# A two-layer hybrid decoder step: block order at three stage starts, and the last squares of a norm summed on PE

## What is computed

```
def _rmsnorm(x, g):
    return x * rsqrt(mean(x * x) + 1e-6) * g
h = _rmsnorm(x, norm_mix_pre)
z = h @ w_in                       # 55 tiles of 128 columns
m = sigmoid(ga) * (ya @ w_out_a) + sigmoid(gb) * (yb @ w_out_b)
x = x + _rmsnorm(m @ w_o, norm_mix_post)
h = _rmsnorm(x, norm_ffn_pre)
f = (silu(h @ w_ffn_gate) * (h @ w_ffn_up)) @ w_ffn_down
x = x + _rmsnorm(f, norm_ffn_post)
```

## Time and profile before

| | us |
|---|---|
| median of 3 runs | 1325.74 |
| lowest and highest | 1322.05, 1326.98 |
| profiled execution, its own time | 1322.61 |
| its span, first to last instruction | 1320.8 |
| PE busy | 1248.3 (95%) |
| DVE, ACT, POOL busy | 866.6, 545.4, 108.2 |
| mean granted PE clock | 0.978 |

### The profile page before, as it was taken

The page is one execution under the profiler, slowest core; times in us unless marked ns, Lnnn a source line. Parts: engine busy times, 40 slices in busy tenths (PEclk is TensorE's granted clock), DMA queues, the critical chain, the costliest instruction groups (busy, mean ns, idle before and its releaser), DMA issues.

```text
span 1320.8 us, 27667 instructions
## 1 busy us (share of the span) xinstructions
PE 1248.3 (95%) x11984; PEld 1174.5 (89%) x11984; DVE 866.6 (66%) x1460; ACT 545.4 (41%) x821; POOL 108.2 (8%) x124
## 2 busy tenths in 40 slices
PE   6999989999998999999989997999999989999996
PEld 5898877899997999999888986879989979999996
DVE  4887558777676566554477873578777656666533
ACT  5552334354445433343444533353434454333432
POOL 0004163000000000000000050720000000000000
PEclk9999989999998999999989999999999989999998
DMA  6433135544453544544423323264444534444541
GB/s 223 128 114 114 52 100 162 176 160 143 136 153 107 183 147 147 154 153 150 143 87 121 117 96 79 71 213 156 144 144 136 160 99 140 160 144 145 158 146 70
DMA packets 51177, 179.50 MB, mean 136 GB/s; under 512 B 6257, under 2 KB 7025, under 8 KB 49777
## 3 DMA queue, kind: packets, MB, share of 16 engines
q1 hardware_dynamic: 41904, 150.49, 36.3%
q10 hardware_dynamic: 9152, 27.25, 6.2%
HBM read 166.57 MB, written 8.53 MB: 133 GB/s over the span
## 4 chain that ended last, share of the span: by engine, by line
PE 83%; DVE 10%; issue 3%; ACT 3%; ACTq 1%; DMA 0%; SPq 0%; DVEq 0%
PE dense L1297 51%; PE core L1297 32%; DVE w_lo L841 2%; ACT w_hi L547 1%; DVE x L889 1%; DVE y_out L887 1%; ACTq L681 1%; DMA x<-x_t 0%; DVE s_gate L1104 0%; DVE s_st L1086 0%; DVE bonus L952 0%; DVE s_st L1087 0%; DVE u_exp L1031 0%; DVE y_a L1151 0%; DVE tmp L938 0%
## 5 line engine op out<-in xcount | busy, mean ns | idle before, releaser
L841 DVE TENSOR_TENSOR w_lo<-w_raw,w_hi 128x1024 fp32r<-128x1024 f32 x282 | 348.8, 1238 | 238.0 <-ACT w_hi L547 237.2
L547 ACT ACTIVATE w_hi<-w_raw 128x1024 fp32r<-128x1024 f32 x282 | 298.0, 1057 | 481.9 <-PE dense L1297 335.3
L1297 PE MATMUL dense<-h_hi,w_hi 128*128 128x320 f32 x1296 | 421.7, 325 | 26.1 <-DVE h_lo L845 14.5
L1297 PE MATMUL dense<-h_lo,w_hi 128*128 128x320 f32 x1296 | 407.1, 314 | 0.0
L1297 PE MATMUL dense<-h_hi,w_lo 128*128 128x320 f32 x1296 | 407.0, 314 | 0.0
L1297 PEld LDWEIGHTS dense<-h_hi,w_hi 128*128 128x128 f32 x1296 | 249.4, 192 | 43.6 <-issue 31.6
L1297 PEld LDWEIGHTS dense<-h_lo,w_hi 128*128 128x128 f32 x1296 | 249.9, 193 | 2.0 <-issue 0.2
L1297 PEld LDWEIGHTS dense<-h_hi,w_lo 128*128 128x128 f32 x1296 | 249.2, 192 | 0.0
L1297 PE MATMUL core<-h_hi,w_hi 128*128 128x320 f32 x416 | 129.8, 312 | 0.0
L1297 PE MATMUL core<-h_hi,w_lo 128*128 128x320 f32 x416 | 129.3, 311 | 0.0
L1297 PE MATMUL core<-h_lo,w_hi 128*128 128x320 f32 x416 | 129.3, 311 | 0.0
(11 more groups left out here) (293 smaller groups left out, 1974.9 us busy)
## 6 DMA issues: line engine op xcount, KB each, us to landing
w_raw<-wts SPq DMA_DIRECT2D x282, 512.0 KB, 3.5
ret_t<-ret_t ACTq DMA_DIRECT2D x16, 256.0 KB, 3.8
ret_s<-ret_t ACTq DMA_DIRECT2D x16, 256.0 KB, 2.4
ret_rest<-ret_d ACTq DMA_DIRECT2D x2, 1536.0 KB, 7.6
qk_rot<-qk_raw ACTq DMA_DIRECT2D x8, 320.0 KB, 6.5
dmask<-rconst ACTq DMA_DIRECT2D x2, 1152.0 KB, 7.1
s_st<-wkv_st ACTq DMA_DIRECT2D x2, 1024.0 KB, 6.0
wkv_s<-s_st ACTq DMA_DIRECT2D x2, 1024.0 KB, 4.4
```

What stands on the lines that cost most here:

```text
L547: act.activation(w_hi[n % RING][:, :], w_raw[n % RING][:, :], ACT.Copy).then_inc(hi_ready.sem, 1)
L841: dve.tensor_tensor(w_lo[r][:, :], w_raw[r][:, :], w_hi[r][:, :].bitcast(F32), ALU.subtract).then_inc(low_made.sem, 1)
L1297: return pe.matmul(out, lhsT, rhs, start=start, stop=stop)
```

## The change

1. **Sums of a norm.** DVE adds seven squares only. PE sums `acc` and then, in a second matmul into the same bank, the eighth square itself. On ACT the `high` behind block 7 moves behind the root. On DVE the `low` of block 7 moves from before the wait for the root to behind the third group of `x`, and `h_lo` of blocks 2 and 3 is made in that place too, one group earlier than before.
2. **Feed-forward.** In the first four cycles of each layer PE takes block k for groups 0, 2, 1, 3 and then block k+1 for the four.
3. **Layer 1's opening** has an order of its own: blocks 0 to 3 of tiles 0 and 1 in turn, blocks 0 to 3 of tile 2, blocks 4 to 7 of tile 0, both sums, blocks 4 to 6 of tile 1, the pick, its block 7, and blocks 4 to 7 of tile 2. Layer 0's and W_OUT_B's orders are written as a list too and stay as they were.
4. **Tile 3 of layer 1.** ACT makes its `w_hi` between the two waits of the root, DVE its `w_lo` before it waits for the root.

```diff
+OPEN_FIRST = [(step - 2 * i, i) for step in range(12) for i in range(3) if 0 <= step - 2 * i < 8]
+OPEN_FIRST[6:6] = [("sum", 0), ("sum", 1)]
+OPEN_FIRST[11:11] = [("pick", 0)]
+OPEN_NEXT = [(k, i) for k in range(4) for i in range(2)] + [(k, 2) for k in range(4)] + [(k, 0) for k in range(4, 8)] \
+    + [("sum", 0), ("sum", 1), (4, 1), (5, 1), (6, 1), ("pick", 0), (7, 1)] + [(k, 2) for k in range(4, 8)]
...
                 def x_root(k):
                     act.wait_ge(*x_partial(layer, k))
                     act.activation(acc[:, :], core[0][:, 0:T], ACT.Copy).then_inc(x_parted.sem, 1)
+                    if k == 1 and layer:
+                        high(RING)
                     act.wait_ge(*x_summed(layer, k))
...
-                        high(after(c))
+                        if c < KT - 1:
+                            high(after(c))
+                    norm_root(k)
+                    high(after(KT - 1))
...
                         dve.wait_ge(*y_squared(layer, (k - 1) * KT + c + 1))
-                        if c:
+                        if 0 < c < KT - 1:
...
-                        for n in lows(c):
-                            low(*n)
+                        if c < KT - 1:
+                            for n in lows(c):
+                                low(*n)
                     dve.wait_ge(*rooted(layer, k))
...
                         if after:
-                            while done < lo:
+                            while done < (hi if i == 2 else lo):
                                 after(done)
                                 done += 1
+                            if i == 2:
+                                for n in lows(KT - 1):
+                                    low(*n)
...
-                    low(layer, j + RING)
+                    if j or not layer:
+                        low(layer, j + RING)
...
+                if layer:
+                    low(layer, RING)
                 dve.wait_ge(*x_rooted(layer, 1))
...
                 def norm_sum(k):
                     pe.wait_ge(*squares(layer, k))
-                    mm(core[0][:, 0:T], ones, acc[:, :]).then_inc(sum_done.sem, 1)
+                    mm(core[0][:, 0:T], ones, acc[:, :], True, False)
+                    pe.wait_ge(*y_squared(layer, k * KT))
+                    mm(core[0][:, 0:T], ones, ch(sq8, KT - 1), False, True).then_inc(sum_done.sem, 1)
...
-                    for ph, one in enumerate((0, 2, 1, 3)):
-                        if k0 == 0:
+                    both = [(one, k) for one in (0, 2, 1, 3) for k in (k0, k0 + 1)]
+                    if ready:
+                        both.sort(key=lambda u: u[1])
+                    for one, k in both:
+                        if k == 0:
                             open_bank(g + one)
```

More of the change, by code:

```diff
@@ L29 @@
 FIRST_WEIGHTS = (0, 2, 3)
-SUMS_AT = (4, 6)
+OPEN_FIRST = [(step - 2 * i, i) for step in range(12) for i in range(3) if 0 <= step - 2 * i < 8]
[3 more added lines that the diff above has]
+    + [("sum", 0), ("sum", 1), (4, 1), (5, 1), (6, 1), ("pick", 0), (7, 1)] + [(k, 2) for k in range(4, 8)]
 X_GROUP_OF = [i for i, (a, b) in enumerate(X_GROUPS) for _ in range(a, b)]
@@ L135 @@
 FILL = (2, 2, 1)
-ACT_STEPS, DVE_STEPS, POOL_STEPS = 13, 221, 18
+ACT_STEPS, DVE_STEPS, POOL_STEPS = 13, 219, 18
 def program(nc, x_t, wts, pvec, lora, shift0, fixed, rmask, trig, rconst, wkv_st, ret_d, ret_t,
@@ L793, in _, with project_out @@
                 high(T_WO + 2 - 1)
-                def project_out(before, after, group0, gain):
+                def project_out(before, after, group0, gain, k):
                     for c in range(8):
@@ L802, in project_out @@
                         act.activation(ch(y_out, c), bank(g)[:, 0:T], ACT.Copy, scale=vec(gain, c)).then_inc(dense_evac_a.sem, 1)
-                        high(after(c))
+                        if c < KT - 1:
+                            high(after(c))
+                    norm_root(k)
+                    high(after(KT - 1))
                 for s in (shift_stored, wkvs_stored, wkvp_stored, retp_stored, *rets_stored):
                     act.wait_ge(*s(layer, s.per_layer))
-                project_out(lambda c: T_WO + c + 2, lambda c: T_WO + c + RING, G_WO, "mix_post")
-                norm_root(1)
+                project_out(lambda c: T_WO + c + 2, lambda c: T_WO + c + RING, G_WO, "mix_post", 1)
                 open_x(layer, 2, "ffn_pre", lambda c: act.wait_ge(*x_mixed(layer, X_GROUP_OF[c] + 1)))
@@ L825, in down_tile @@
                     return T_DOWN + (FK * (c + 1) - 1) // KT
-                project_out(lambda c: down_tile(c) + 2, lambda c: down_tile(c) + 3 if c == 7 else down_tile(c) + 2, G_DOWN, "ffn_post")
-                norm_root(2)
+                project_out(lambda c: down_tile(c) + 2, lambda c: down_tile(c) + 3 if c == 7 else down_tile(c) + 2, G_DOWN, "ffn_post", 2)
                 assert steps[0] == ACT_STEPS, steps
@@ L874, in norm_add @@
                         dve.wait_ge(*y_squared(layer, (k - 1) * KT + c + 1))
-                        if c:
+                        if 0 < c < KT - 1:
                             ins = dve.tensor_tensor(acc[:, :], ch(sq8, 0) if c == 1 else acc[:, :], ch(sq8, c), ALU.add)
-                            if c < KT - 1:
+                            if c < KT - 2:
                                 link(ins)
@@ L1354, in x_pick, with opening @@
                     mm(core[0][:, 0:T], pick, acc[:, :]).then_inc(x_summed.sem, 1)
[L1356 to L1379, removed]
+                def opening(j0, g0, ready, first, order):
+                    for k, i in order:
+                        j, g = j0 + i, g0 + i
+                        if k == "sum":
+                            x_sum(1, i)
+                            continue
+                        if k == "pick":
+                            x_pick(1)
+                            continue
+                        if k == 0:
+                            pe.wait_ge(*low_ready(layer, j))
+                            open_bank(g)
+                        if i == 0:
+                            pe.wait_ge(*ready(layer, first + k + 1))
+                        for n, (w, which) in enumerate(parts(j, k)):
+                            ins = mm(bank(g)[:, 0:T], w, ch((h_hi, h_lo)[which], k), k == 0 and n == 0, k == KT - 1 and n == 2)
+                        if k == KT - 1:
+                            ins.then_inc(tile_used.sem, 1)
+                opening(0, 0, h_ready, 0, OPEN_NEXT if layer else OPEN_FIRST)
                 pe.wait_ge(*lora_loaded(layer, 1))
@@ L1709, in _ @@
                                      for k in range(4)], ya_hi, ya_lo)
-                opening(T_WOB, G_WOB, yb_ready, 0)
+                opening(T_WOB, G_WOB, yb_ready, 0, [u for u in OPEN_FIRST if u[0] not in ('sum', 'pick')])
                 for c in range(RING, 8):
@@ L1719, in cycle @@
                     pe.wait_ge(*low_ready(layer, T_GU + n))
-                    for ph, one in enumerate((0, 2, 1, 3)):
-                        if k0 == 0:
-                            open_bank(g + one)
[L1723 to L1728, removed]
+                    both = [(one, k) for one in (0, 2, 1, 3) for k in (k0, k0 + 1)]
+                    if ready:
+                        both.sort(key=lambda u: u[1])
+                    for one, k in both:
+                        if k == 0:
+                            open_bank(g + one)
+                        if ready and one == 0:
+                            pe.wait_ge(*ready(layer, k))
+                        for m, (w, which) in enumerate(parts(T_GU + n, 4 * (k - k0) + one)):
+                            ins = mm(bank(g + one)[:, 0:T], w, ch(act[which], k), k == 0 and m == 0, k == last and m == 2)
+                        if k == k0 + 1:
+                            ins.then_inc(phase_done.sem, 1)
                 for q in range(FK // 2):
```

## The result

The kernel after takes 1313.5 us in the median of 4 runs (1311.33 to 1314.26), the kernel before 1325.9 (1322.05 to 1326.98) beside it. The ratio is 0.9922 with an interval from 0.9902 to 0.9941: 10.3 us, from 7.8 to 13.0. A second measurement with more runs gave 0.9926 (0.9909 to 0.9942), 9.8 us. The forecast was 7.0 us faster, or 1318.7 us, in a range from 1314.5 to 1323.0, and faster by over 0.5% was its likeliest case. The way was right.

What follows compares the result with a forecast made beforehand. PE bounds the kernel, busy 1248.3 of 1320.8 us, so gains lie where it stands still or runs slowly. 0.5 + 2.1 + 2.1 + 2.3 = 7.0 us off the 1325.74 median gives 1318.7, range 1314.5 to 1323.0.

Steps and rivals of the forecast that it cites:

- Start of the chain: Four norm ends: the sum of `acc` fits behind the last tile, so the second sum starts 0.52 us earlier at each.
- The gap in the feed-forward: Feed-forward starts: PE's wait for block 1, worth 1.19 us, goes; block 4 is in time with 1.9 us in hand.
- The clock's term: Feed-forward starts: clock rises 5.1 to 6.0 us after an earlier last restart; 2.1 us gained each, gap and earlier root included.
- My bounds, 0.9 and 2.35: Gain per feed-forward start: 0.9 us if the clock rises no earlier than before, 2.35 if 5.1 us after the restart.
- The opening: Layer 1's start: two gaps become one of 0.2 us and the clock rises earlier; gain 2.3 us, bounds 1.4 and 2.8.
- my own list: Signs for and against; the prediction is wrong if, among others, PE waits for `h_lo` of block 4 or later.
- rival (b): Moved `w_lo` delays DVE's blocks 4 to 7, `acc` sum doesn't fit; gain only 4.8 us, 1320.9; chance 0.17.
- The sum: Whole kernel: 0.5 (end) + 2.1 + 2.1 (feed-forward starts) + 2.3 (layer 1's opening) = 7.0 us faster.
- upper bound of 8.05: Whole kernel, largest gain: 0.55 + 2.35 + 2.35 + 2.8 = 8.05 us, or 1317.7 us.
- Rival (a): At the three starts the clock rises no earlier although PE runs without gaps; gain 3.7 us, 1322.0; chance 0.17.
- Rival (c): Stalls elsewhere now drop the clock; 16 us more slow time cancels the gain, 30 more give 1332; chance 0.04.
- The 20 us of slow time elsewhere: Slow clock outside the three starts, some 20 us now, would have to more than double for the kernel to become slower.

Runs made afterwards that it cites:

- without_sum: The kernel after with the norm's new sum and all that was moved with it put back; ratio to the kernel before 0.9944 (0.9922 to 0.9965).
- after_fill3: The kernel after with three matmuls that nobody reads added behind the norm's sum; ratio to the kernel before 0.9944 (0.9925 to 0.9962).
- open_alone: The kernel before with only layer 1's new opening order and tile 3's halves made before the root; ratio 0.9971 (0.9958 to 0.9984), 3.8 us.

## Why the prediction came out right, and where it was off

- **Start of the chain, right.** The root and `y_out` came 0.5 us earlier at each end; the sum of `acc` fit behind the last tile; the tail gave 0.52.
- **The gap in the feed-forward, right.** PE doesn't stop in the first cycles, and the `h_lo` of block 4 is 1.2 us early (1.9 forecast; it ends at about 423.8, and PE comes at 424.99).
- **The clock's term, right in direction, too small.** I took the clock to be low at PE's restart, as in the three places before, and to rise 5 to 6 us later. In the kernel after it fell only 1.35 us behind the restart (416.92 against 415.57), and was slow for 3.4 us instead of 10.2, all of it behind the restart, where I had 5.6. The start gained 3.2 us instead of 2.1; 0.45 x (5.6 - 3.41) = 1.0 is this difference. This is the term of the sum that was mis-sized. The second execution had 6.8 us of slow clock at the first start, 5.53 of it behind the restart, and gained 2.25 there, which is my figure. At full clock on either side the two orders, edit 1 included, are 24.43 - 22.85 = 1.58 us apart, more than the 1.15 at equal low clock, since the old order then waits longer for block 1 (1.29 us); the rest of 3.2 is clock. My bounds, 0.9 and 2.35, were too narrow above: they moved the rise and left the fall where it was, and the rise came earlier too, 4.75 us behind the restart and not 5.1 or more.
- **The opening, 2.65 for 2.3, inside its bounds.** I had seen that `h_lo` would set a floor, but put it at block 7 with 0.6 us in hand at block 4. The `h_lo` of block 4 came nearly when I said (8.2 us behind PE's restart, I had 8.4); PE was ready for it earlier (8.1, I had 9.0), and waited. By my own list a wait for block 4 was a sign of being wrong. It came true here, and it bounds this term.
- **Edit 1 is not worth 0.5 at every end.** It gave 0.52 at the tail and 0.5 at each feed-forward start at equal low clock, but not in layer 1. I had put the moved `w_lo` into DVE's chain and taken it to fit. It makes `h_lo` of block 4 come 1.25 us later against the cut than without edit 1, and so the opening can't be shorter than 48.4. With the old orders, where PE wants that block after 18 matmuls, it cost 1.2 us more than the kernel before there. This is the first half of rival (b)'s mechanism, hidden by the other gains; its second half, that the sum of `acc` doesn't fit, is refuted.
- **The sum.** 7.0 forecast; 9.5 by stretches. Of the 2.5 between them 2.2 are from the two feed-forward starts and 0.35 from the opening. That the sum lies beyond my upper bound of 8.05 and the time still near the range is luck in part: the range was widened by the spread of the runs.
- **Rival (a)**, a rise no earlier, is refuted: the clock rose 4.75 us behind the restart of the first start (420.32 - 415.57), 7.97 before (425.36 - 417.39), and all starts in the new order agree (3.7 to 5.5). **Rival (c)**, slow clock elsewhere, is real as an effect: the unchanged mixing stretch took 353.4 to 359.9 us, and this execution of the kernel after had 358.9, 2.5 more than before's. The clock was low for 13.7 us in that stretch then, for 10.2 us in before, and for 6.8 us in the second execution of the kernel after, which had 355.2. So this doesn't hang on the change. (The 20 us of slow time elsewhere that the prediction gives leave out some 8 us at the kernel's end.)

The Trainium skill (TensorE: Matmul & The Clock Gate, Part 1: The HAM clock gate) says that the moment of the clock's change isn't tied to the kernel. These runs agree: the same kernel's first feed-forward start had 3.4 us of slow clock in one execution and 6.8 in the other, 0.95 us apart.

What stays open: how much of the 10 us is edit 1's. The times say 0.9926 with it and 0.9944 without, 2.4 us with overlapping intervals, but from two measurements. The one measurement that has both kinds gives 0.9944 for without_sum and 0.9944 for after_fill3, whose stretches are those of the kernel after: nothing. The stretches say 1.2 us (0.6 + 0.6 + 0.5 - 0.5), or 1.8 (0.6 + 0.6 + 0.5 + 0.1) where the low clock in the opening is as long as in open_alone. No measured time shows edit 1's share.

## What to carry to other kernels

Where an engine restarts on pieces that arrive one by one, order its work so that the first pieces feed as many results as there are banks: it fills the gaps, and with TensorE's clock that pays twice. The matmul order of the feed-forward alone took 3.4 us off the time here. A step moved out of one wait lands in front of something else; follow that engine's queue to the piece that is wanted latest, not only past the first one. If TensorE must wait some microseconds before a dense stretch, matmuls that nobody reads can be cheaper than the wait, if they fill nearly all of it: six helped here and three did not.

## What the runs showed of the hardware

- A wait of 3.7 to 4.3 us on TensorE at the kernel's norms was followed by 3.4 to 10.2 us at the low clock, in every trace without filler; with six filler matmuls (0.5 us of waiting left) the clock stayed at 1.00 in both feed-forward starts, and in the kernel after in the opening too. With three (2.11 us left) it fell for 3.4 us at each of the three places. In the kernel before with six it fell for 3.4 us in the opening, where PE also waits 1.29 and 1.35 us for blocks 1 and 2.
- The fall can come after the restart: 1.35 us behind it in the kernel after, 2.3 us ahead of it in the kernel before (415.12 against 417.39). The low time behind the restart cost 0.45 us for each microsecond.
- Two float32 passes behind a dense stretch began 0.15 us behind the last matmul, and the next pair 0.69 us later (410.35, 411.04): they cost the chain nothing.
